# Rotary embedding in two mixers: rows exchanged by small SBUF-to-SBUF transfers instead of TensorE products

## The reference, cut to what matters

```
def apply_partial_rope(x, cos, sin):
    half = ROPE_DIM // 2          # ROPE_DIM = 16 of the 64 numbers of a head
    x1, x2 = xf[..., :half], xf[..., half:ROPE_DIM]
    out = jnp.concatenate([x1 * c - x2 * s, x2 * c + x1 * s, xf[..., ROPE_DIM:]], axis=-1)
```

## Time and profile before

| | us |
|---|---|
| median of 3 runs | 2500.43 (2499.33 to 2500.62) |
| the profiled execution, its own time | 2499.81 |
| its span in the trace | 2497.7 |
| TensorE busy in the span | 2466.7 (99%) |
| VectorE busy | 2081.8 (83%) |
| ScalarE busy | 1591.4 (64%) |
| GpSimd busy | 202.6 (8%) |

### The profile page before, as it was taken

The page is one execution under the profiler, slowest core; times in us unless marked ns, Lnnn a source line. Parts: engine busy times, 40 slices in busy tenths (PEclk is TensorE's granted clock), DMA queues, the critical chain, the costliest instruction groups (busy, mean ns, idle before and its releaser), DMA issues.

```text
span 2497.7 us, 44188 instructions
## 1 busy us (share of the span) xinstructions
PE 2466.7 (99%) x17236; PEld 2250.9 (90%) x17236; DVE 2081.8 (83%) x2845; ACT 1591.4 (64%) x2345; POOL 202.6 (8%) x275
## 2 busy tenths in 40 slices
PE   9999999999999999999999999999999999999999
PEld 9999998999999999999998799988899899997998
DVE  5688857999999999999999699785898798786665
ACT  5644556888888888888887644557544544566543
POOL 2111021000000000000000111013111011013000
PEclk9999999999999999999999999999999999999999
DMA  7698545999999999999999588443687587432542
GB/s 290 233 359 318 194 166 211 395 364 381 366 378 367 375 371 374 371 373 372 371 375 380 219 305 318 161 144 110 235 320 293 218 324 290 149 128 76 219 178 76
DMA packets 136637, 696.21 MB, mean 279 GB/s; under 512 B 16528, under 2 KB 16656, under 8 KB 87728
## 3 DMA queue, kind: packets, MB, share of 16 engines
q1 hardware_dynamic: 109872, 598.79, 64.3%
q0 software_dynamic: 23424, 88.16, 9.2%
q10 hardware_dynamic: 3136, 6.43, 0.7%
HBM read 683.28 MB, written 13.24 MB: 279 GB/s over the span
## 4 chain that ended last, share of the span: by engine, by line
PE 90%; DVE 6%; ACT 2%; issue 1%; POOL 1%; DVEq 0%; ACTq 0%; POOLq 0%
PE ps L2384 16%; PE ps L1967 15%; PE ps L1968 15%; PE ps L1969 15%; PE ps L2546 12%; PE ps L2386 8%; DVE w_parts L1691 1%; PE ps L1995 1%; PE ps L2516 1%; DVE w_parts L1333 1%; PE ps L1991 1%; DVE a_parts L1699 1%; ACT w_parts L1119 1%; ACT w_parts L794 0%; DVE xT L1355 0%
## 5 line engine op out<-in xcount | busy, mean ns | idle before, releaser
L2384 PE MATMUL ps<-a_parts,w_parts 128*128 128x512 f32 x1760 | 618.5, 393 | 0.3
L1691 DVE TENSOR_TENSOR w_parts<-ring,w_parts 128x1024 fp32r<-128x1024 f32 x448 | 548.5, 1224 | 52.9 <-ACT w_parts L1119 50.6
L1967 PE MATMUL ps<-w_parts 128*112 128x256 f32 x1792 | 515.4, 288 | 0.0
L1969 PE MATMUL ps<-w_parts 128*112 128x256 f32 x1792 | 498.6, 278 | 0.0
L1968 PE MATMUL ps<-w_parts 128*112 128x256 f32 x1792 | 498.5, 278 | 0.0
L2386 PE MATMUL ps<-a_parts,w_parts 128*128 128x256 f32 x1760 | 492.6, 280 | 0.0
L1119 ACT ACTIVATE w_parts<-ring 128x1024 fp32r<-128x1024 f32 x448 | 472.0, 1054 | 0.0
L2384 PEld LDWEIGHTS ps<-a_parts,w_parts 128*128 128x128 f32 x1760 | 329.8, 187 | 73.5 <-issue 2.8
L2386 PEld LDWEIGHTS ps<-a_parts,w_parts 128*128 128x128 f32 x1760 | 332.3, 189 | 0.0
L1967 PEld LDWEIGHTS ps<-w_parts 128*112 128x112 f32 x1792 | 313.0, 175 | 11.8 <-issue 0.2
L1968 PEld LDWEIGHTS ps<-w_parts 128*112 128x112 f32 x1792 | 312.6, 174 | 11.8
(11 more groups left out here) (272 smaller groups left out, 4519.1 us busy)
## 6 DMA issues: line engine op xcount, KB each, us to landing
ring<-wstream SPq DMA_DIRECT2D x378, 1024.0 KB, 7.3
ring<-wstream SPq DMA_DIRECT2D x378, 512.0 KB, 6.0
proj<-astream POOLq DMA_DIRECT2D x144, 512.0 KB, 5.7
slot_rows<-branch POOLq DMA_DIRECT2D x7, 448.0 KB, 6.9
slot_out<-slot_rows POOLq DMA_DIRECT2D x1, 3136.0 KB, 14.8
sq<-slot_rows ACTq DMA_DIRECT2D x49, 64.0 KB, 5.5
slot_out<-pT ACTq DMA_DIRECT2D x49, 64.0 KB, 5.3
vtok<-crow POOLq DMA_DIRECT2D x3, 512.0 KB, 4.0
```

The lines of the kernel that those rows point to most:

```text
L1691: nc.vector.tensor_tensor(up_lo[:, n % 2, at], ring[:, s, at], up_hi[:, n % 2, at], ALU.subtract)\
L1967: mm(o, stationary[0], moving[0], start=start, stop=False, skip_group_check=True)
L1969: return mm(o, stationary[1], moving[0], start=False, stop=stop, skip_group_check=True)
L2384: mm(ps[:, bank, :], hi, a_parts[:, :, k, :], start=k == 0, stop=k == KB - 1, skip_group_check=True)
```

## The change

The product with `rot` goes, with its constant, its semaphore and `ROPE_JOBS`. In its place GpSimd's queue issues transfers from `proj` to `hT` that copy rows 8 to 15 of each head to rows 0 to 7 and the reverse. There are three groups (`SWAPS`): blocks 8 to 12, blocks 0 to 3, blocks 4 to 7. Each group is four transfers (two heads, two directions) of 8 partitions: 5120 bytes per partition in the first, 4096 in the others. The sign moves into the sine table. VectorE reads the exchanged rows from `hT` in SBUF, where it read PSUM. VectorE and GpSimd wait for all four transfers of a group. GpSimd's order is: group 0, cosines of steps 0 to 2, group 1, group 2, cosines of steps 3 to 6. ScalarE's squares of queries and keys, which write `hT`, wait for step 2.

```diff
-ROPE_JOBS = {4: (0,), 5: (1,), 6: (2,), 17: (3,), 18: (4,), 19: (5,), 20: (6,)}
+SWAPS = ((8, 5), (0, 4), (4, 4))
...
+        def swap_tile(b, w):
+            return hT[:, b % 8:b % 8 + w, :]
+        def swap_of(b):
+            return 0 if b >= KB else 1 + b // 4
...
             def ropes(m):
-                n = len(PAIRS) * (m - 2)
-                for i, (b, w) in enumerate(PAIRS):
-                    pool.wait_ge(rot_ready, n + i + 1)
+                l = m - 2
+                n = len(PAIRS) * l
+                def swap(g):
+                    b, w = SWAPS[g]
+                    if b < KB:
+                        pool.wait_ge(qk_ready, 8 * l + b + w)
+                    else:
+                        pool.wait_ge(in_copied, UNITS_BEFORE[m] + b - 8 + w)
+                    for h in range(0, P, HD):
+                        for half in range(2):
+                            dst, src = h + 8 * half, h + 8 * (1 - half)
+                            pool.dma_start(swap_tile(b, w)[dst:dst + 8, :, :], proj[src:src + 8, b:b + w, :])\
+                                .then_inc(swapped[g], 16)
+                def turn(i):
+                    b, w = PAIRS[i]
+                    pool.wait_ge(swapped[swap_of(b)], 64 * (l + 1))
                     nc.gpsimd.tensor_tensor(proj[:, b:b + w, :], proj[:, b:b + w, :],
                                             C("cos").unsqueeze(1).broadcast_to([P, w, T]), ALU.mult)\
                         .then_inc(cos_ready, 1)
+                swap(0)
+                for i in range(3):
+                    turn(i)
+                swap(1)
+                swap(2)
+                for i in range(3, len(PAIRS)):
+                    turn(i)
...
             def key_squares(m):
                 act.wait_ge(in_copied, UNITS_BEFORE[m] + 15)
+                act.wait_ge(rope_ready, len(PAIRS) * (m - 2) + 3)
...
                     n = len(PAIRS) * l + i
-                    dve.wait_ge(rot_ready, n + 1)
+                    dve.wait_ge(swapped[swap_of(b)], 64 * (l + 1))
...
-                        term, ps[:, 7 - i % 2, 0:w * T].rearrange("p (b t) -> p b t", t=T),
+                        term, swap_tile(b, w),
                         C("sin").unsqueeze(1).broadcast_to([P, w, T]), ALU.mult))
...
-                for j in ROPE_JOBS.get(n, ()):
-                    if j == 3:
-                        pe.wait_ge(root_ready, 2 * (l + 1))
-                    b, w = PAIRS[j]
-                    i = len(PAIRS) * l + j
-                    if b < KB:
-                        pe.wait_ge(qk_ready, 8 * l + b + w)
-                    else:
-                        pe.wait_ge(in_copied, before + b - 8 + w)
-                    if i >= 2:
-                        pe.wait_ge(rope_ready, i - 1)
-                    mm(ps[:, 7 - j % 2, 0:w * T], C("rot"), proj[:, b:b + w, :], start=True, stop=True)\
-                        .then_inc(rot_ready, 1)
...
-            cos[h + a], sin[h + a] = np.cos(ang[:, a % 8]), np.sin(ang[:, a % 8])
+            cos[h + a], sin[h + a] = np.cos(ang[:, a % 8]), (1 if a >= 8 else -1) * np.sin(ang[:, a % 8])
```

More of the change, by code:

```diff
@@ L91 @@
 _at = 0
-for _n, _w in (("ident", P), ("headmean", P), ("rot", P), ("after", P),
+for _n, _w in (("ident", P), ("headmean", P), ("after", P),
                ("cmask0", P), ("cmask1", T),
@@ L331, in build @@
         qk_ready = sem("qk_ready")
-        rot_ready = sem("rot_ready")
+        swapped = [sem(f"swapped{i}") for i in range(len(SWAPS))]
         root_ready = sem("root_ready")
@@ L2688, in _constants @@
     put("headmean", np.where(i[:, None] // HD == i[None, :] // HD, 1.0 / HD, 0.0))
[L2690 to L2695, removed]
     put("after", (i[:, None] > i[None, :]).astype(np.float32))
```

## The result

The changed kernel takes 2515.91 us (median of 4 runs, 2514.80 to 2517.86) against 2500.52 (2499.33 to 2501.28): a ratio of 1.0068, 95% interval 1.0056 to 1.0079 (the quotient of the two medians, 1.0062, lies within it). It is slower, by 15.4 us, and by more than the 2504.6 that I forecast. The profiled execution took 2517.86 us with a span of 2515.8, 18.1 us more than the span before.

A forecast was written before the change was run, and what follows sets the result against it. TensorE was taken to bound each `mixer2` call to about 1662, then VectorE's order. TensorE's gain less group 2's issues and port waits gave +2.1 us a call, doubled to +4.2: 2504.6 us, 8-in-10 range 2498.5 to 2511.

The forecast's parts named there:

- the shift: Change of the moment VectorE reaches `divided(u+1)` in each `mixer2` call; +1.1 to +3.6 us, taken as +2.1.
- What bounds the stretch: In `mixer2`, TensorE sets the pace to about 1662, then VectorE's order to 1684.67; at most 2.15 us saved counts.
- Landing of group 0: Before step 0: the transfers land 3.3 us after the last issue begins, with 2.2 and 6.0 kept as ends.
- g = 1.2: How much earlier TensorE lets the low part of tile 7 start: 1.2 us, ends 2.15 and -0.6.
- Who waits for group 0: After step 0: indexer products, before at 1621.82, would come at 1619.7, just covered; low part of tile 4 covered too.
- Rival 3: Group 0 lands 6 us or more after issue, behind the weight tile; each call 1.8 us later, 2508.2; chance 0.17.
- Group 2's issues ahead of cosine 3: Four GpSimd issues, 2.2 us, delay cosine 3; add of step 3 can't begin before 1662.9, against 1661.26 before.
- The second case: Steps 3 and 4: cosines follow each other without giving way, so VectorE's adds and sine wait; late by 4.1 us.
- The first case of the sum: Steps 3 and 4: the port goes to whoever waits; VectorE late by 1.6 to 2.9 us.
- rival 5: TensorE's clock falls from 2.4 to 1.2 GHz in standstills up to `turned(u+1)`; some 3 us a call, 2510; chance 0.05.
- rival 4: GpSimd's SBUF-to-SBUF issue costs 1 us, not 0.54; up to 3.2 us a call, 2511; chance 0.08.
- Rival 1: TensorE is the bound throughout and all 11.2 us come back: 2489.2; chance 0.08.

The follow-up runs named there:

- the split group: Changed kernel with group 0 cut into blocks 8-9 and 10-12, weight tile's load waiting for the second part, cosines 3-4 before blocks 4-7's issues: 2498.67 us.
- the filled waits: Changed kernel with small unread products filling TensorE's three longest waits, after units 7, 20 and 21: 2515.33 us.
- the kernel with the cosines first: Changed kernel with cosines 3 and 4 placed before group 2's issues in GpSimd's order: 2509.98 us.
- the kernel with all waits filled: Changed kernel with small unread products after units 7, 20 and 21, plus two pairs ahead of scores(u+3) and turned(u+1): 2514.97 us.

## Why the prediction was wrong

The direction and the places were right; the shift was taken as +2.1 us a call and is +7.8 at D, +9.4 at the end of the call. By the prediction's own steps:

- **What bounds the stretch.** Right. In no version did the removed 11.2 us come back. With everything mended (the split group), TensorE is early by the full 2.15 us up to tile 7, and VectorE's order up to D ends last, as read from the earlier trace rows. (TensorE was not busy for 5.00 of 5 us in all windows up to 1680: the first, from 1590, has 4.90. Nothing rests on it.)
- **Landing of group 0: the step that failed.** I took 3.3 us from the last issue, between 2.2 and 6.0, with the argument that 160 KB are little beside a weight tile. The last of them took 7.3, beyond both ends, and 6.2 to 8.0 in all ten calls. With the tile's load held back they took 2.7, the low part of tile 7 came 1.22 us earlier than before (g = 1.2 was predicted), D was 2.90 later (2.1 predicted; in the second call the two are 0.66 and 3.41), and the time 5.6 us over the kernel before (4.2 predicted). So the rest of the sum was good for a group with no tile issued just ahead of it, and this term, with what it set off, was worth 9.8 of the 15.4 us. I had the 92% and read them as a share of time; what counted was what had been issued just ahead, the 1.5 MB of 1604.37 and 1604.74. At the 292 GB/s of that window they need 5.4 us by themselves. Nor were the 160 KB little: in the windows of 1 us in which the group was in flight with the tile held back (1605 to 1607), the DMA engines were busy for 0.48 and 0.59 at only 90 and 106 GB/s, where the four such windows after 1607 beside the tile have 0.94 to 0.99 at 307 to 369.
- **Who waits for group 0.** I watched the indexer products, with 2.1 us to spare. The first to be held up was the low part of tile 3, which stands behind step 0 in VectorE's order, and with it TensorE at unit 8, 4.31 us. Less the 2.15 us of products that are gone that is 2.2. After it the products of unit 8 started 0.21 us apart until 1623.2 and 0.12 from there on, 13 of them, which is 1.3 us more; together 3.5, and the low part of tile 7 was late by 3.73. That 1.3 was not all on the path: filling the wait gave back only about 0.4 us (the stretch from the first sine to the low part of tile 7 is 42.89 us after, 42.46 with the filled waits), since TensorE then waits 0.7 us for the rotation at the indexer products. How much of it is price of the wait alone shows where the group landed nearly as early as my own 6.0: in the first call of the kernel with the cosines first it took 6.2, and tile 7 was late by 2.8, where I had 0.6. So what a late landing costs was mis-sized too, not only the landing.
- **Rival 3** was this mechanism, and it decided, though its threshold of 3.4 us was not tested (no landing lies between 3.2 and 6.2 us in the two kinds of runs). It was priced at 1.8 us a call from a landing of 6 us and without the wait at unit 8.
- **Group 2's issues ahead of cosine 3.** Right: 1.98 us of issues (2.16 forecast), and the add of step 3 waits 3.10 us (some 2.7 forecast).
- **Who gets the port.** The second case came true for the adds: cosine 4 follows cosine 3 at once and the add that waits for cosine 3 takes 1.71 us, 1.02 more than alone; the one of step 4 takes 1.63. The sine of step 4 was hardly held (0.79 us). From the low part of tile 7 to that of tile 8 the stretch grew by 4.61 us (10.30 to 14.91); the sum had 2.1 + 1.2 = 3.3, and for this case 5.3. The 0.5 us that come back at step 5 were there too: from tile 8 to D it is 18.16 us, before 18.70. (The first case of the sum, by its own rows, is 1.5 to 2.8 us and not 1.6 to 2.9.)
- **The clock (rival 5)** did fall after standstills, where I gave it 0.05. In the trace that is 1.56 us a call behind D, half of what the rival had; in the time it could not be told.
- **The issue's price (rival 4)**, 1 us, was wrong: 0.50, below the 0.54 of the earlier trace rows. Rival 1, all 11.2 us back, was wrong by 26.7 us.
- **The chances.** 0.47 for slower was right, but the range ended at 2511 since each rival was added to the sum alone. Late landing, the port's second case and the clock came together. The first two are separate causes that add up, as the runs show; the falls of the clock follow the longer waits.

The Trainium skill (DMA: Bandwidth & Descriptors, the section on queues, rings and completion order) says that each DMA engine goes round-robin between the queues with work, packet by packet. By that rule a group of 160 KB would get about half of the 292 GB/s beside a tile and be through in about 1 us plus the fixed part, an estimate of some 3 us. The time disagrees with that estimate: the last transfer took 7.3 us from GpSimd's queue and 5.4 from ScalarE's. The order of the landings (three transfers of the group ahead of the tile's first half, the last beside its second half) speaks for a service that mixes the two, as the rule has it, so it is the half share that did not come true and not necessarily the turns. The measurement decides; why the group's share was smaller is not shown by any run.

The Trainium skill (SBUF — State Buffer, the shared port pair) has the lock held for a whole instruction, and the trace agrees: 1.71 us for an add of 0.69, 4.52 for a low part of 3.41. In most calls the order is plain: the end of cosine 3 lets both go, and cosine 4 starts at about 1667.0 (1665.74 + 1.3), the add at 1667.16. What the traces add is that a GpSimd instruction right behind another can get in ahead of a VectorE instruction that already waits: the add of 4.16 us stood there through cosines 4, 5 and 6. It isn't so each time; in the second call of the kernel with all waits filled the add took 1.70 us with four cosines in 5.95. What decides between the two is not shown.

Open: whether a version exists that keeps the 2.15 us of tile 7 up to D (the split group keeps 0.27 and 1.03 of it). It would have to place the four late cosines beside neither `qk_scaled` nor a low part; I did not try it. And what sets the difference between the two calls of one run (12.4 and 14.2 us to the first sine).

## What to carry to other kernels

Before a small transfer is put on the path, look up in SyncE's timeline what was issued in the microseconds ahead of it: here it landed together with that bulk, not after its own size. If it must be quick, hold the bulk load back until it has landed; here that one wait was worth 9.8 us, and no engine's wait for the held tile shows in the two calls. Removing work from the engine that is 99% busy is worth only as much as the next engine's order can take up: ask at the stage's end which engine is the later one, and price the in-order queue that the new instructions go into, with everything behind them.

## What the hardware showed that I had not expected

- The last of four transfers of 40 KB (8 partitions) from SBUF to SBUF took 7.3 us (6.2 to 8.0 in ten calls) with a 1.5 MB load issued 0.8 to 1.1 us ahead of the first, and 2.7 us with that load held back (3.2 in the second call). One of 32 KB took 2.0 us in a quiet stretch.
- GpSimd needs 0.50 us for each issue of 32 or 40 KB, nearly as much as the 0.54 us for 512 KB; ScalarE needed 0.63 us for each of the same four, except the first of the first call with 1.25.
- An add that waits for the first of two GpSimd cosines in a row took 1.66 to 1.71 us where it takes 0.69 alone, in every call but two; in those two it took 4.16 us and let three cosines pass.
- After 4.3 us of standstill the granted clock was 0.67 in the next window of 5 us at 4.70 us of work; with small products in the wait it stayed 1.00.
